# Sparse attention in pairs of heads: v held stationary, outputs by features

## The reference

```python
s = jnp.einsum('bsghd,bngd->bghsn', q, kc) * NSA_SCALE          # compressed: n = 31
p = masked_softmax(s, end[None, :] <= t[:, None])
o = jnp.einsum('bghsn,bngd->bsghd', p.astype(vc.dtype), vc)
...
s = jnp.einsum('bqghd,bkgd->bghqk', qi, ks) * NSA_SCALE         # selected, window
p = masked_softmax(s, mask).astype(vs.dtype)
return jnp.einsum('bghqk,bkgd->bqghd', p, vs)
```

## Time and profile before

| | |
|---|---|
| median of 3 runs | 2802.15 us (2800.6 to 2807.3) |
| the profiled execution | 2802.34 us, span 2800.6 us |
| granted clock of TensorE, mean | 0.992 |
| PE, DVE, ACT, POOL busy | 2767.3, 2006.5, 1155.2, 62.6 us |
| the loop over groups | from about 345 to 677 us of the span |
| share of the chain that ended last: PE, DVE | 77%, 19% |

### The profile page before, as it was taken

How to read it: one execution, slowest core, us unless ns; L and a number is a source line. 1 busy time by engine, 2 the same in 40 slices (tenths; PEclk the granted TensorE clock), 3 DMA queues, 4 the chain that set the end, 5 groups by cost and what they waited for, 6 DMA issues and landing times.

```text
span 2800.6 us, 41644 instructions
## 1 busy us (share of the span) xinstructions
PE 2767.3 (99%) x16832; PEld 2467.0 (88%) x16832; DVE 2006.5 (72%) x2964; ACT 1155.2 (41%) x1635; POOL 62.6 (2%) x22
## 2 busy tenths in 40 slices
PE   8999999999999999999999999999999999999998
PEld 7888888898888989889898899988999888889897
DVE  5456564544668969689694797876978588669795
ACT  4343444444343424434344443432434357434342
POOL 0000011111000000000000000000000000000000
PEclk9999999999999999999999999999999999999999
DMA  7223322322533333323333233322332353123332
GB/s 224 91 79 106 113 68 79 94 82 98 179 129 104 101 104 114 107 91 105 106 106 107 76 105 106 105 94 91 106 117 91 107 192 112 61 75 106 106 106 76
DMA packets 262194, 295.41 MB, mean 105 GB/s; under 512 B 6211, under 2 KB 248019, under 8 KB 259343
## 3 DMA queue, kind: packets, MB, share of 16 engines
q1 hardware_dynamic: 257008, 281.53, 30.9%
q10 hardware_dynamic: 5022, 11.57, 1.1%
HBM read 276.30 MB, written 16.78 MB: 105 GB/s over the span
## 4 chain that ended last, share of the span: by engine, by line
PE 77%; DVE 19%; issue 2%; ACT 1%; DMA 0%; DVEq 0%; ACTq 0%; SPq 0%
PE bank L1451 12%; PE bank L1452 12%; PE bank L1453 12%; PE bank L1918 5%; PE bank L1920 5%; PE bank L1919 5%; PE bank L1746 5%; PE bank L1804 2%; DVE gate_quarters_lo L2726 2%; DVE up_quarters_lo L2726 2%; PE bank L2093 1%; PE bank L1466 1%; PE bank L1468 1%; PE bank L1467 1%; PE bank L1794 1%
## 5 line engine op out<-in xcount | busy, mean ns | idle before, releaser
L2213 DVE TENSOR_TENSOR w_lo<-w_raw,w_hi 128x2048 fp32r<-128x2048 f32 (+2 forms) x140 | 306.4, 2191 | 131.7 <-ACT w_hi L846 128.0
L846 ACT ACTIVATE w_hi<-w_raw 128x2048 fp32r<-128x2048 f32 (+2 forms) x134 | 243.1, 1821 | 237.0 <-PE bank L1453 159.8
L1451 PE MATMUL bank<-hid_hi,w_hi 128*128 128x512 f32 x816 | 317.9, 390 | 0.0
L1452 PE MATMUL bank<-hid_lo,w_hi 128*128 128x512 f32 x816 | 317.6, 389 | 0.0
L1453 PE MATMUL bank<-hid_hi,w_lo 128*128 128x512 f32 x816 | 317.5, 389 | 0.0
L1451 PE MATMUL bank<-h_hi,w_hi 128*128 128x512 f32 x736 | 292.4, 397 | 2.8 <-DVE w_lo L2213 1.7
L1453 PE MATMUL bank<-h_hi,w_lo 128*128 128x512 f32 x736 | 286.9, 390 | 0.0
L1452 PE MATMUL bank<-h_lo,w_hi 128*128 128x512 f32 x736 | 286.8, 390 | 0.0
L1453 PEld LDWEIGHTS bank<-hid_hi,w_lo 128*128 128x128 f32 x816 | 153.2, 188 | 32.1
L1451 PEld LDWEIGHTS bank<-hid_hi,w_hi 128*128 128x128 f32 x816 | 153.2, 188 | 31.4
L1452 PEld LDWEIGHTS bank<-hid_lo,w_hi 128*128 128x128 f32 x816 | 153.2, 188 | 31.2
(11 more groups left out here) (490 smaller groups left out, 7072.6 us busy)
## 6 DMA issues: line engine op xcount, KB each, us to landing
w_raw<-in_ffn_w_in_dram SPq DMA_DIRECT2D x88, 1024.0 KB, 5.0
w_raw<-in_ffn_w_out_dram SPq DMA_DIRECT2D x32, 1024.0 KB, 5.1
w_raw<-in_w_in_dram SPq DMA_DIRECT2D x28, 1024.0 KB, 5.3
w_raw<-in_w_ffn_in_dram SPq DMA_DIRECT2D x22, 1024.0 KB, 5.1
w_raw<-in_ffn_w_out_dram SPq DMA_DIRECT2D x16, 768.0 KB, 4.4
w_raw<-in_conv_w_pw_dram SPq DMA_DIRECT2D x12, 1024.0 KB, 6.9
phase_taps<-in_conv_dw_phases_dram SPq DMA_DIRECT2D x10, 1152.0 KB, 8.0
w_raw<-in_w_ffn_down_dram SPq DMA_DIRECT2D x8, 1024.0 KB, 5.1
```

The lines of the kernel that those rows point to most:

```text
L846: nc.scalar.activation(w_hi[SLOT[u]][:, 0:n], raw[s][:, 0:n], ACT.Copy).then_inc(w_hi_ready, 1)
L1451: nc.tensor.matmul(bank[b][:, 0:n], wh, xh, start=first, stop=False)
L1452: nc.tensor.matmul(bank[b][:, 0:n], wh, xl, start=False, stop=False)
L2213: v.tensor_tensor(w_lo[slot][:, 0:n], raw[s][:, 0:n], w_hi[slot][:, 0:n].bitcast(F32), ALU.subtract).then_inc(w_lo_ready, 1)
```

## The change

The steps are reordered (query block outermost, then branch, then head) and taken in 16 pairs of two heads. TensorE's loop has 19 rounds: round m scores pair m and transposes and weighs pair m - 3 (`BEHIND`), so that eight probability tiles are in flight instead of four; the four new ones lie in halves of the weight tiles of slot 1.

VectorE multiplies the probabilities by gate / row sum before they are transposed (`scale_pair`, in the round before). ScalarE copies the transposed tile as fp32r (`step_high`), VectorE subtracts it from the bank to give the low part (`step_low`), both into one tile for the pair. TensorE then holds v, with its high and low part side by side as 128 columns, stationary, and moves 256 columns, both heads' queries, through it: one matmul for the high part of p, one of 64 columns for the low part (`weigh`). Outputs have features on partitions, high products on the lower and those with v's low part on the upper half of a bank; all three branches of a query block add up in one bank. The compressed branch is one matmul of 512 columns for each query block, its four transposes a third item in the first round of a block. ScalarE copies one half and VectorE adds the other to `ynsa` (`y_copy`, `y_add`), then it is split (`y_high_of`, `y_low`); `y_tok` and its transposes are gone. v is split at the start of each group.

The gate weights come as six units of 128 columns. Each tile has a unit of its own; the number of gate matmuls in a round stands in `GATE_PAIR`, and after which round ScalarE copies a tile or makes a high part in `GATE_EVAC` and `GATE_HIGH`. The last unit that a turn of the loop converts (the next group's unit 0) is converted over the full 2048 columns. q and the keys of the next group are loaded when the last scores are made.

Long runs of removed lines are left out here, since they stand in the listing above.

```diff
-STEPS = [(br, qb, hh) for br in range(2) for qb in reversed(range(TT)) for hh in range(HPG)]
+STEPS = [(br, qb, hh) for qb in reversed(range(TT)) for br in range(2) for hh in range(HPG)]
 NS = len(STEPS)
+PAIRS = NS // 2
+PER_BLOCK = NS // TT
+PAIRS_PER_BLOCK = PER_BLOCK // 2
 S_BANK = (2, 3)
...
+TURN = (5, 6)
+OUT_BANK = (1, 7)
...
+GATE_PAIR = (9,) * 3 + (7,) * 8 + (6,) * 4 + (4,) * 4
+GATE_EVAC = {1: 0, 4: 1, 8: 2, 11: 3, 15: 4}
+GATE_HIGH = {2: 2, 4: 3, 8: 4, 11: 5, 15: 6}
+BEHIND = 3
+PROBS = 8
...
+for _u in range(U_NSA, U_MERGE):
+    WIDTH[_u] = HALF
...
+        prob = [at(f"prob{i}", [P, T], WK + (8 + 2 * i) * KB) for i in range(4)]
+        prob += [at(f"prob{4 + i}", [P, T], W0 + (28 + 16 * (i // 2) + 2 * (i % 2)) * KB) for i in range(4)]
+        pt = [at(f"prob_pair_turned_{part}", [P, TT, 2, P], WK + (16 + 4 * i) * KB, F32R) for i, part in enumerate(("high", "low"))]
+        v_st = at("v_high_low", [P, 2, TT, 2 * DH], WK + 24 * KB, F32R)
         p_c = at("p_cmp", [P, TT, HPG, NC], WK + 28 * KB)
-        pT_c = at("pT_cmp", [NC, TT * HPG, P], WK + 12 * KB)
+        pT_c = at("pT_cmp", [32 + NC, T], WK + 44 * KB, F32R)
+        vc_st = at("v_cmp_high_low", [32 + NC, 2 * DH], WK + 38 * KB + 256, F32R)
...
+                sp.wait_ge(s_s, g * NS + 1)
...
+                def step_high(i):
+                    br, qb, hh = STEPS[i]
+                    j = item_of(i)
                     if i % 2 == 0:
...
+                        act.wait_ge(s_o, g * PAIRS + (i // 2 + 1))
+                    act.wait_ge(s_t, g * ITEMS + (j + 1))
+                    nc.scalar.activation(pt[0][:, 0:qb + 1, hh % 2, :], bank[TURN[j % 2]][:, 0:P * (qb + 1)].rearrange("p (k q) -> p k q", q=P),
+                                         ACT.Copy).then_inc(s_pa, 1)
...
+                def y_copy(o):
+                    qb = TT - 1 - o
+                    act.wait_ge(s_o, g * PAIRS + (PAIRS_PER_BLOCK * (o + 1) + 1))
+                    heads = bank[OUT_BANK[o % 2]][:, :].rearrange("p (t h q) -> p t h q", h=2, q=P)
+                    y = ynsa[1][:, bass.ds(g * 2, 2), qb * P:(qb + 1) * P].bitcast(F32)
+                    nc.scalar.activation(y[0:DH], heads[DH:P, :, 0, :], ACT.Copy)
+                    nc.scalar.activation(y[DH:P], heads[0:DH, :, 1, :], ACT.Copy).then_inc(y_half, 1)
...
+                    act.wait_ge(w_used, g * GATE_TILES + (U_NSA + m + 1))
...
+                for m in range(PAIRS + BEHIND + 2):
+                    k = m - BEHIND
+                    if 0 <= k < PAIRS:
+                        step_high(2 * k)
+                        step_high(2 * k + 1)
+                        if k % PAIRS_PER_BLOCK == 0:
+                            cmp_high(k // PAIRS_PER_BLOCK)
+                    if m < PAIRS:
+                        exp_step(2 * m)
+                        exp_step(2 * m + 1)
+                    if m == 0:
                         act.wait_ge(c_sh, g + 1)
                         nc.scalar.activation(p_c[:, :, :, :], p_c[:, :, :, :], ACT.Exp, scale=DH ** -0.5).then_inc(c_e, 1)
...
+                    if k >= PAIRS_PER_BLOCK and k % PAIRS_PER_BLOCK == 0:
+                        y_copy(k // PAIRS_PER_BLOCK - 1)
+                        if k == PAIRS:
+                            gate_evac(5)
+                    if k >= PAIRS_PER_BLOCK and k % PAIRS_PER_BLOCK == 1:
+                        y_high_of(k // PAIRS_PER_BLOCK - 1)
+                    if m in GATE_EVAC:
+                        gate_evac(GATE_EVAC[m])
+                    if m in GATE_HIGH:
+                        n = GATE_HIGH[m]
+                        high_in_loop(g * (GATE_TILES // 2) + (U_NSA // 2 + n // 2), n % 2, n % 2, HALF if n < GATE_TILES else UNIT)
...
-                for n in range(4):
-                    low_in_loop(g * 4 + (U_NSA + 1 + n), (n + 1) % 2, HALF if n in (1, 2) else UNIT)
+                for n in range(1, GATE_TILES + 1):
+                    low_in_loop(g * GATE_TILES + (U_NSA + n), n % 2, HALF if n < GATE_TILES else UNIT)
...
                 def turn(i):
                     br, qb, hh = STEPS[i]
...
+                    pe.wait_ge(p_scaled, g * NS + (i + 1))
+                    out_ = turn_bank(item_of(i))
                     for kb in range(qb + 1):
-                        ins = nc.tensor.transpose(bank[5 + i % 2][:, kb * P:(kb + 1) * P], prob[i % 4][:, kb * P:(kb + 1) * P], ident)
+                        ins = nc.tensor.transpose(out_[:, kb * P:(kb + 1) * P], prob[i % PROBS][:, kb * P:(kb + 1) * P], ident)
                     ins.then_inc(s_t, 1)
 
...
+                def cmp_turn(o):
+                    pe.wait_ge(c_p, g + 1)
+                    out_ = turn_bank(cmp_item(o))
+                    for hh in range(HPG):
+                        ins = nc.tensor.transpose(out_[0:NC, hh * P:(hh + 1) * P], p_c[:, TT - 1 - o, hh, :], ident)
+                    ins.then_inc(s_t, 1)
+                def weigh(k):
+                    o, r = divmod(k, PAIRS_PER_BLOCK)
+                    br, qb, hh = STEPS[2 * k]
+                    out_ = bank[OUT_BANK[o % 2]]
+                    if r == 0:
+                        pe.wait_ge(v_parts, g + 1)
+                        if o >= 1:
+                            pe.wait_ge(s_or, g * TT + (TT + o - 1))
+                        pe.wait_ge(s_pd, g * ITEMS + (cmp_item(o) + 1))
+                        nc.tensor.matmul(out_[:, :], vc_st[:, :], pT_c[:, :], start=True, stop=False)
+                    else:
+                        pe.wait_ge(s_pd, g * ITEMS + (item_of(2 * k + 1) + 1))
+                    c = hh * P
                     for kb in range(qb + 1):
-                        ins = nc.tensor.matmul(bank[OUT_BANK[i // HPG % 2]][:, c:c + DH], probT[i % 4][:, kb * P:(kb + 1) * P],
-                                               v_sw[br][:, kb, bass.ds(g * DH, DH)], start=kb == 0, stop=kb == qb)
+                        last = r == PAIRS_PER_BLOCK - 1 and kb == qb
+                        nc.tensor.matmul(out_[0:DH, c:c + 2 * P], v_st[:, br, kb, 0:DH], pt[1][:, kb, :, :].rearrange("p h q -> p (h q)"),
+                                         start=False, stop=False)
+                        ins = nc.tensor.matmul(out_[:, c:c + 2 * P], v_st[:, br, kb, :], pt[0][:, kb, :, :].rearrange("p h q -> p (h q)"),
+                                               start=False, stop=last)
                     ins.then_inc(s_o, 1)
 
...
+                for m in range(PAIRS + BEHIND):
+                    k = m - BEHIND
+                    if m < PAIRS:
+                        scores(2 * m)
+                        scores(2 * m + 1)
+                    if k == 0:
                         pe.wait_ge(m_lo_s, 4)
...
+                    if k >= 0:
+                        turn(2 * k)
+                        turn(2 * k + 1)
+                        if k % PAIRS_PER_BLOCK == 0:
+                            cmp_turn(k // PAIRS_PER_BLOCK)
+                    gates(GATE_PAIR[m])
+                    if k >= 0:
+                        weigh(k)
...
+                dve.wait_ge(s_o, g * PAIRS + 1)
...
+                def scale_pair(k):
+                    br, qb, hh = STEPS[2 * k]
+                    n = P * (qb + 1)
+                    if k % 2 == 0:
+                        four = slice(2 * k, 2 * k + HPG)
+                        dve.wait_ge(s_e, g * NS + (2 * k + HPG))
+                        link(v.reciprocal(prec[:, four], psum_row[:, four]))
+                        link(v.tensor_tensor(cg[:, four], prec[:, four], gate4[:, qb, bass.ds(g * HPG, HPG), br + 1], ALU.mult))
+                    for i in (2 * k, 2 * k + 1):
+                        v.tensor_scalar(prob[i % PROBS][:, 0:n], prob[i % PROBS][:, 0:n], cg[:, i:i + 1], None, ALU.mult).then_inc(p_scaled, 1)
+                def step_low(i):
+                    br, qb, hh = STEPS[i]
+                    j = item_of(i)
+                    dve.wait_ge(s_pa, g * ITEMS + (j + 1))
+                    v.tensor_tensor(pt[1][:, 0:qb + 1, hh % 2, :], bank[TURN[j % 2]][:, 0:P * (qb + 1)].rearrange("p (k q) -> p k q", q=P),
+                                    pt[0][:, 0:qb + 1, hh % 2, :].bitcast(F32), ALU.subtract).then_inc(s_pd, 1)
...
+                def y_add(o):
+                    qb = TT - 1 - o
+                    dve.wait_ge(y_half, g * TT + (o + 1))
+                    heads = bank[OUT_BANK[o % 2]][:, :].rearrange("p (t h q) -> p t h q", h=2, q=P)
+                    y = ynsa[1][:, bass.ds(g * 2, 2), qb * P:(qb + 1) * P].bitcast(F32)
+                    for h in range(2):
+                        half = slice(DH * h, DH * (h + 1))
+                        ins = v.tensor_tensor(y[half], y[half], heads[half, :, h, :], ALU.add)
                     ins.then_inc(s_or, 1)
 
...
+                cmp_max()
+                for m in range(PAIRS + BEHIND + 2):
+                    k = m - BEHIND
+                    if m < PAIRS:
+                        mask_step(2 * m)
```

(19 more changed lines are left out.)

259 lines of the change are left out of this document (89 added, 170 removed).

## The result

The changed kernel takes 2847.72 us (median of 4 runs, 2843.74 to 2852.73), the kernel before 2802.76 (2800.6 to 2807.3) beside it: ratio 1.0159, 95% interval [1.0137, 1.0181]. It is slower by 45 us. The forecast was slower by 11, 2813, with a range up to 2836: the sign is right, the size four times too small.

The account below looks back on a forecast made before the run. TensorE bounds the group loop: 69.1 us work, 14.6 idle and 1.4 half clock give 85.1 a group against 82.1. Four groups +12, first group -1: 2802.3 + 11 = 2813 us; 8-in-10 range 2774 to 2836.

Parts of the forecast that it names:

- Forecast idle 14.6 us a group: Loop over four key groups: sum of TensorE's waits for ScalarE and VectorE, 14.6 us on 69.1 of work.
- The compressed transposes: Rounds 3, 7, 11, 15: third item waits for a bank to be copied and subtracted, 3.75 us idle a group.
- ScalarE late behind its gate work: From rounds 8 and 11, gate copies and high parts delay ScalarE's turned copies by 0.55 and 1.0 us.
- the lock in round 12: GpSimd's low weight part holds VectorE's factor product on SBUF operands: 1.05 us of TensorE idle.
- the two tail waits: Group's end: 2.7 us idle for ScalarE's full-width high part, then 4.1 for factors held by GpSimd's full-width low part.
- small misfits: Elsewhere in a group's rounds: 1.4 us of TensorE idle not assigned to a named wait.
- The q and key loads are now issued after the last scores ... Both nothing; if q were late it would cost up to 2 us a group.: Group ends: loads have the whole tail to land, so cost nothing; a late q up to 2 us a group.
- again seven gate matmuls, 1.4 us; bounds 0 and 3: Tail of each group: one half-clock stretch as before the change, 1.4 us a group, between 0 and 3.
- slower still: Rival: pairs lose 0.25 us each in hand-offs, or clock also falls in rounds 11 to 14; kernel 2830; chance 0.14.
- TensorE's own work: Each group: 23.1 us removed, 10.1 added, net 13.0 less; TensorE alone would need 69.1 us.
- Scalings beside GpSimd: Rounds 5 and 9: if the skill's rule holds, odd pairs' scalings are held too, 0.2 to 0.9 us a group more.
- Faster: Rival: the tail's two waits do not arise; group 76.9 us, kernel 2781, or 2770 with half the misfits; chance 0.24.

Follow-up runs that it names:

- e2_low_tiny: Changed kernel with GpSimd converting only 8 columns of each gate weight's low part in the groups: 2819.21 us, ratio 1.0058 to the kernel before.
- e4_half: Changed kernel with each group's last conversion at half width, the other half converted after the loop: 2840.88 us, ratio 1.0136 to the kernel before.
- e5_start: Changed kernel with SyncE, not VectorE, making the first steps of counts s_s and s_or: 2830.75 us, ratio 1.0106 to the kernel before.
- e11_before_late_q: Kernel before, with only the first step of c_t, which releases the q load, moved to VectorE's end of work ahead: 2819.71 us, ratio 1.0063.
- e3_fill: Changed kernel plus useless TensorE matmuls in the two waits at each group's end, rounds 16 and 17: 2838.64 us, ratio 1.0127 to the kernel before.
- e10_between: e9_early with unit 5's conversion moved to round 12 and gate products moved between rounds: 2794.41 us, ratio 0.9970 to the kernel before.
- e7_all: e5_start plus v's low parts made after round 1's compressed weights, last conversion half width in round 18, its rest behind the loop: 2811.49 us, 1.0032.
- e1_q_first: Changed kernel with SyncE, not VectorE, making the first step of s_s that releases the q load: 2840.71 us, ratio 1.0134 to the kernel before.
- e9_early: e7_all plus four gate products ahead of compressed transposes, and unit 1's high part made at the end of the group before: 2801.41 us, 0.9994.

## Why the prediction was too small

**The stage and the bound held.** Forecast idle 14.6 us a group, measured 14.6, 12.7, 14.8; that the first agrees to the tenth is luck, as the waits that the prediction named come to about 12 instead of 13.2 and one that it did not name adds 2.2. The compressed transposes (3.75, measured 3.2), ScalarE late behind its gate work (0.55 and 1.0, measured 0.53 and 1.07), the lock in round 12 (1.05, measured 0.8) and the two tail waits (2.7 and 4.1, measured 2.75 and 3.6 to 3.9) are in the trace where the instruction lists put them, and e2_low_tiny and e4_half separate their causes as stated: L1843 the lock, L1869 ScalarE's width. The prediction listed 1.4 as "small misfits"; what stands there is 0.5 at L1863 and the 2.2 at L1809 in two groups of three. It had not seen that v's split is such an instruction too.

**The step that failed first: "The q and key loads are now issued after the last scores ... Both nothing; if q were late it would cost up to 2 us a group."** That is right for groups 2 to 4 and left out group 1, where no scores stand ahead: there the count's first step is what releases the load, and the diff moves that step from SyncE to VectorE (`sp.sem_inc(c_t, 1)` goes, `dve.sem_inc(s_s, 1)` comes). The term put at nothing cost 17 us (e5_start, e11_before_late_q): a wait of 14.65 and the half clock behind it. No rival had it.

**The step that failed second: the clock, "again seven gate matmuls, 1.4 us; bounds 0 and 3".** Measured 6.2, 4.2 and 5.8 us a group by halving. Two errors: the stretch behind the tail is 5.3 us long, not 3, and there are two or three a group, not one: also behind the 1.05 + 0.8 us of rounds 12 and 13 and behind the first mask's 2.2. The stretch before the change was no model for it: before, the one stretch a group stood behind 3.7 us in which TensorE was never idle. The rival "slower still" named the clock in rounds 11 to 14 and gave it 0.14. In the three groups that is 12.0 us more. e3_fill shows the tail's part of it directly, 2.2 us, where halving gives 3.0.

**A small size: TensorE's own work.** Forecast 69.1 us a group at full clock, measured 71.5 to 71.8, 2.5 more, although the 256-column matmuls start 0.12 apart as forecast. In e10_between, at full clock, TensorE is busy 73.6, so that the split between clock and work above is good to 2 us a group. Part of the difference is waiting that does not show as idle, because a gate matmul is shown 0.39 us long and its successor could start after 0.23: in e10_between one at 534.73 is followed by the weighing at 535.16, just as VectorE's low part ends (535.11). At the 12 weighings behind a gate matmul of one such group this comes to 1.9 us over the 0.23 and the idle shown. The rest I have not taken apart.

**The sum.** Between the profiled spans lie 47.5 us. 11 were forecast; the three groups took 273.3 us where 3 x 85.1 = 255.3 were (12.0 by the clock, 7.6 by the work, less 1.7 in idle), 18 more; the first load 17 by the medians. That is 46. With the 22 us between the profiled executions of e5_start and of the changed kernel in place of the 17 it is 51, and TensorE begins the merge products 49.2 us later than before (726.58 against 677.41); so the sum closes within 2 us up to there, and the unchanged stages behind were 1.7 us quicker in this execution.

**Scalings beside GpSimd.** In the changed kernel two full-width scalings took 1.45 us while GpSimd was converting (486.10 to 488.51), and two of 384 columns in round 9 took 1.66 (GpSimd 504.42 to 506.79) where they take 0.75 alone. Two full-width ones with no conversion beside them, and then the two of 487.75:

```profile
483.94 0.88 DVE L2553 TENSOR_SCALAR prob<-prob,nsa_stat 128x512 f32<-128x512 f32 x2
487.75 1.45 DVE L2553 TENSOR_SCALAR prob<-prob,nsa_stat 128x512 f32<-128x512 f32 x2
```

In e7_all a one-input copy was held to 1.78 us. The Trainium skill, page "SBUF — State Buffer", section "Who interferes with whom", says that a tensor_scalar in a two-port mode locks against GpSimd as well; the traces agree. The prediction set 0.2 to 0.9 us a group beside its sum for this; VectorE lost 0.57 + 0.91 in the group, but TensorE shows no wait of 0.2 us or more for a scaling in those two rounds.

**"Faster" was not absurd.** Its condition, the tail's idle under 3 us, is what e7_all to e10_between make true; its 2781 was not reached, since TensorE is busy 73.6 us a group and not 69.1.

## What to carry to other kernels

When a count is given a new meaning, ask for its first turn who makes the first step and when: a load that is early in every later turn can be 21 us late in the first. Price an idle stretch of TensorE twice, as the wait and as what the matmuls behind it lose at half the clock, which here was 1.5 to 3 us behind waits of 2 to 4 and about 8 behind one of 14.6; filling the wait with useless matmuls recovered the second of the two (e3_fill). Compare the moment at which the changed stage ends, and not only the spans: the unchanged 2122 to 2126 us behind it differed by 5 us between executions. And before a change is dropped, take away its waits one by one: the same matmuls, with conversions, first counts and gate products in other places, went from 1.6% slower to 0.3% faster.

## What the runs showed of the hardware

- The length of the half-clock stretch follows the idle ahead of it only loosely: 16.6 us behind 14.65 idle, at least 16.5 behind 6.6 (e1_q_first), 5.3 behind 2.75 + 3.62, 3.3 behind 2.18.
- The same wait does not always bring it. Behind the first mask's 2.17 to 2.18 the clock fell in two groups of two in the changed kernel and in none of the three of e1_q_first and e3_fill that have this wait. Behind single waits of 1.0 to 1.4 in e9_early and e10_between the clock stayed at 1.00 in groups 2 and 3; behind 1.05 + 0.8 it fell in four groups of four in the changed kernel, in three of four in e3_fill and in one of four in e9_early.
- Idle is not the only thing ahead of a half-clock stretch: in the kernel before it stands behind 3.70 us of which TensorE was busy 3.70.
- A two-input VectorE instruction on SBUF operands waited out the whole of a GpSimd instruction that had started 0.14 us earlier and was not touched by one that started 0.02 us later; one with an operand in PSUM, or the masks, ran through (0.87 for two at 553.60, beside GpSimd's 553.38 to 555.84).
- A VectorE that turns from one group to the next without any named wait took 3.3 to 3.5 us in the changed kernel, the DMA engines 4% busy, and 5.7 in e9_early, the DMA engines 66% busy with weights.
